# The first norm of a diffusion step: six scale tiles on TensorE ahead of the products, two as row sums on VectorE, the norm's factor applied on GpSimd, loads in another order

## The reference, cut to what matters

```
m = (silu(cond) @ mod_w[i] + mod_b[i]).reshape(.., 9, 1024)        # for c_ctx and for c
x = rms_norm(h, norm_g) * (1 + m[3j+1]) + m[3j]                    # scale, shift
h += 0.5 * m[3j+2] * ((silu(x @ w_gate) * (x @ w_up)) @ w_down)    # hidden width 2816
```

## Time and profile before

| what | us |
|---|---|
| median of 3 runs | 1693.14 (1692.27 to 1697.59) |
| profiled execution | 1691.21 |
| its span | 1689.4 |
| TensorE, matmuls busy | 1616.0 |
| VectorE busy | 1005.7 |
| ScalarE busy | 575.3 |
| GpSimd busy | 84.5 |

### The profile page before, as it was taken

The page is one execution under the profiler, slowest core; times in us unless marked ns, Lnnn a source line. Parts: engine busy times, 40 slices in busy tenths (PEclk is TensorE's granted clock), DMA queues, the critical chain, the costliest instruction groups (busy, mean ns, idle before and its releaser), DMA issues.

```text
span 1689.4 us, 23807 instructions
## 1 busy us (share of the span) xinstructions
PE 1616.0 (96%) x9348; PEld 1559.3 (92%) x9348; DVE 1005.7 (60%) x1338; ACT 575.3 (34%) x738; POOL 84.5 (5%) x48
## 2 busy tenths in 40 slices
PE   5799999989799989999999999998999998999999
PEld 5799999989655889999998999998999998999999
DVE  4667677857645666766875767687755435333323
ACT  3233332252245353323234323213643325232321
POOL 1200000025200010000010000001000000000000
PEclk9599999989779989999998999999999998999999
DMA  9445445625300335454654454466432332333332
GB/s 369 96 175 200 172 174 205 242 80 192 128 0 1 116 121 203 179 194 174 227 196 150 172 201 177 163 233 233 148 142 100 125 125 98 127 124 124 125 124 87
DMA packets 58233, 262.81 MB, mean 156 GB/s; under 512 B 15678, under 2 KB 16574, under 8 KB 36286
## 3 DMA queue, kind: packets, MB, share of 16 engines
q1 hardware_dynamic: 58174, 262.00, 42.9%
HBM read 259.68 MB, written 2.29 MB: 155 GB/s over the span
## 4 chain that ended last, share of the span: by engine, by line
PE 86%; DVE 6%; DMA 3%; issue 2%; ACT 2%; POOL 1%; SPq 0%; POOLq 0%; DVEq 0%; ACTq 0%
PE ps L961 16%; PE ps L962 16%; PE ps L964 16%; PE ps L935 8%; PE ps L936 7%; PE ps L937 7%; DVE mprod L659 3%; DMA raw<-panels 2%; PE ps L974 2%; PE ps L977 2%; PE ps L975 2%; PE ps L1118 2%; PE ps L1023 1%; PE ps L1153 1%; ACT w_hi L459 1%
## 5 line engine op out<-in xcount | busy, mean ns | idle before, releaser
L651 DVE TENSOR_TENSOR w_lo<-raw,w_hi 128x2048 fp32r<-128x2048 f32 x164 | 375.7, 2292 | 294.6 <-ACT w_hi L459 293.8
L961 PE MATMUL ps<-x_hi,w_hi 128*128 128x384 f32 x1536 | 523.9, 341 | 19.5 <-DVE x_lo L729 10.8
L962 PE MATMUL ps<-x_hi,w_lo 128*128 128x384 f32 x1536 | 522.4, 340 | 0.0
L964 PE MATMUL ps<-x_lo,w_hi 128*128 128x384 f32 x1536 | 519.8, 340 | 0.0
L459 ACT ACTIVATE w_hi<-raw 128x2048 fp32r<-128x2048 f32 x169 | 322.9, 1911 | 339.5 <-PE ps L937 191.6
L659 DVE SCALAR_TENSOR_TENSOR mprod<-mraw,cB 128x1024 f32<-128x1024 f32 x256 | 316.9, 1238 | 7.4
L961 PEld LDWEIGHTS ps<-x_hi,w_hi 128*128 128x128 f32 x1536 | 292.4, 190 | 23.4 <-issue 12.1
L962 PEld LDWEIGHTS ps<-x_hi,w_lo 128*128 128x128 f32 x1536 | 292.7, 191 | 0.0
L964 PEld LDWEIGHTS ps<-x_lo,w_hi 128*128 128x128 f32 x1536 | 292.5, 190 | 0.0
L935 PE MATMUL ps<-act_hi,w_hi 128*128 (+1 forms) x832 | 279.8, 336 | 0.3 <-DVE w_lo L651 0.3
L937 PE MATMUL ps<-act_hi,w_lo 128*128 (+1 forms) x832 | 279.7, 336 | 0.0
(11 more groups left out here) (135 smaller groups left out, 1190.0 us busy)
## 6 DMA issues: line engine op xcount, KB each, us to landing
raw<-panels SPq DMA_DIRECT2D x169, 1024.0 KB, 4.8
mraw<-mod_rows SPq DMA_DIRECT2D x128, 512.0 KB, 3.6
mscale<-mod_scale SPq DMA_DIRECT2D x8, 512.0 KB, 15.7
mshift<-mod_rows SPq DMA_DIRECT2D x8, 512.0 KB, 15.9
bias<-toep_scratch SPq DMA_DIRECT2D x32, 64.0 KB, 2.9
h<-x_in_t SPq DMA_DIRECT2D x1, 1536.0 KB, 8.4
out<-h SPq DMA_DIRECT2D x4, 384.0 KB, 2.3
cB<-cond_rows SPq DMA_DIRECT2D x1, 1024.0 KB, 5.4
```

What stands on the lines that cost most here:

```text
L651: nc.vector.tensor_tensor(w_lo[q0 % 2][:, :], raw[q0 % 2][:, :], w_hi[q0 % 2][:, :].bitcast(F32), ALU.subtract).then_inc(lo_done, 1)
L961: mm(out, hi[:, cols], x_hi[:, k, :], start=(k == 0), stop=False)
L962: mm(out, lo[:, cols], x_hi[:, k, :], start=False, stop=False)
L964: last = mm(out, hi[:, cols], x_lo[:, k, :], start=False, stop=(k == KD - 1))
```

## The change

Scale tiles 0 to 5 stay on TensorE and go ahead of all products: tiles 0 and 1 before the sums of squares, tile 2 between them and the spread, tiles 3 to 5 behind it. They lie three to a PSUM bank, and VectorE takes them over in two groups of three (`from_pe`). Scale tiles 6 and 7 become row sums on VectorE (`late`), from rows of `mod_rows`. Shift sums start ahead of the norm (tiles 0 to 2), one stands inside it (tile 3), the others between the splits and the subtractions. [...] Panels 0 and 1 share four tiles of x instead of three. The loads start with scale tile 0 and h, ahead of `cB`; panels 0 and 1 come after k = 3 and k = 5. The row sums write to `mprod0`, which shares its place with the bias, so `load_bias` moves behind pair g0 = 2 and waits for the first sums.

```diff
+PE_TILES = 6
+SUM_TILES = 2 * KD - PE_TILES
@@ SyncE, pair
-                    if f == 0 and g0 == 1:
+                    if f == 0 and g0 == 2:
+                        sp.wait_ge(mchain, 2 * SUM_TILES)
                         load_bias()
@@ SyncE, start
+            def mod_first(k):
+                sp.dma_start(mscale[:, k, :], mod_scale[k] if k < PE_TILES else mod_rows[KD + k]).then_inc(mscale_in[k], 16)
+                sp.dma_start(mshift[:, k, :], mod_rows[k]).then_inc(mshift_in[k], 16)
+
+            sp.dma_start(mscale[:, 0, :], mod_scale[0]).then_inc(mscale_in[0], 16)
+            sp.dma_start(h[:, :, :], x_in_t).then_inc(x_in, 16)
             sp.dma_start(cB[:, :, :], cond_rows.rearrange("(o c) k -> o c k", o=1).to_broadcast([P, 2, D])).then_inc(cb_in, 16)
+            sp.dma_start(mshift[:, 0, :], mod_rows[0]).then_inc(mshift_in[0], 16)
             sp.dma_start(vec[:, :], vecs).then_inc(vec_in, 16)
             sp.dma_start(ident[:, :], consts[0]).then_inc(const_in, 16)
-            sp.dma_start(h[:, :, :], x_in_t).then_inc(x_in, 16)
-            for k in range(KD):
-                sp.dma_start(mscale[:, k, :], mod_scale[k]).then_inc(mscale_in[k], 16)
-                sp.dma_start(mshift[:, k, :], mod_rows[k]).then_inc(mshift_in[k], 16)
-                if k < 2:
-                    panel(k, 0)
+            for k in range(1, KD):
+                mod_first(k)
+                if k in (3, 5):
+                    panel(k // 2 - 1, 0)
@@ GpSimd
             norm(0)
+            pool.wait_ge(r_done, 1)
+            for k in range(KD):
+                if k >= 4:
+                    pool.wait_ge(x_done, k - 3)
+                nc.gpsimd.tensor_tensor(tmp[:, k % 4, :], h[:, k, :], sq[:, 3, :], ALU.mult).then_inc(t_done, 1)
@@ ScalarE
             split(0, 0)
+            act.wait_ge(rb_done, 1)
+            nc.scalar.activation(sq[:, 3, :], ps[:, 5, 0:T], ACT.Copy).then_inc(r_done, 1)
             split(1, 0)
             make_x(0, (0, 0))
@@ VectorE (row_sums waits for a tile's load and calls cond_sums, which now writes to mprod0)
-            rms(0)
+            def first_scale(ks, scale):
+                n = ks.stop - ks.start
+                link(nc.vector.tensor_tensor(aT[:, ks, :], scale, mb1[:, ks, None].to_broadcast([P, n, 2]), ALU.add))
+                nc.vector.tensor_tensor(aT[:, ks, :], aT[:, ks, :], ngT[:, ks, None].to_broadcast([P, n, 2]), ALU.mult) \
+                    .then_inc(mvec, n)
+            def late(k):
+                row_sums(mscale[:, k, :], mscale_in[k], scsum[:, k - PE_TILES, :])
+                shift_sums(k)
+            shift_sums(0)
+            shift_sums(1)
+            shift_sums(2)
+            rms(0, beside=lambda: shift_sums(3))
+            first_shift(slice(0, 4))
+            from_pe(0)
             split(0, 0)
             split(1, 0)
-            make_x(0, first_mod)
+            shift_sums(4)
+            low(0)
+            shift_sums(5)
+            low(1)
+            first_shift(slice(4, 6))
+            from_pe(1)
+            low(2)
+            late(6)
+            late_vectors(6)
+            low(3)
+            low(4)
+            late(7)
+            late_vectors(7)
+            for k in range(5, KD):
+                low(k)
@@ TensorE
-                        project_first(feature_major, q, (0, 2), n,
-                                      (lambda k: mod_scale_tile(k + 1) if 0 < k < KD - 1 else None) if f == 0 else lambda k: None)
+                        project_first(feature_major, q, (0, 2), n, 3 if f else 4)
@@ TensorE, start
+            mod_scale_tile(0)
+            mod_scale_tile(1)
             pe.wait_ge(const_in, 16)
             pe.wait_ge(ones_set, 2)
             norm_sums(0)
+            mod_scale_tile(2)
             norm_spread(0)
-            mod_scale_tile(0)
-            mod_scale_tile(1)
+            for k in range(3, PE_TILES):
+                mod_scale_tile(k)
```

More of the change, by code:

```diff
@@ L82, in build @@
         shsum = sb("shsum", [P, KD, 2])
+        scsum = sb("scsum", [P, KD - PE_TILES, 2])
         cB = sb("cB", [P, 2, D])
@@ L114, in build @@
             svb = sb("svb", [P, KS, T], scope=s)
+        with ExitStack() as s:
+            mprod0 = sb("mprod0", [P, D], scope=s)
         with ExitStack() as s:
@@ L178, in build @@
         rb_done = sem("rb_done")
+        r_done = sem("r_done")
         t_done = sem("t_done")
@@ L298, in mod_block @@
                     if b0 > MOD_FIRST or not isinstance(ii, int):
-                        sp.wait_ge(mchain, 2 * KD + 2 * MT * (b0 - MOD_FIRST - 1) + 2 * a + 2 + 2 * MT * ii)
+                        sp.wait_ge(mchain, 2 * SUM_TILES + 2 * MT * (b0 - MOD_FIRST - 1) + 2 * a + 2 + 2 * MT * ii)
                     sp.dma_start(mraw[a][:, :], mod_rows[bass.ds(MT * (b0 + ii) + a, 1), :, :].rearrange("a p k -> p (a k)")) \
@@ L652, in split, with cond_sums @@
                                         ALU.subtract).then_inc(lo_done, 1)
-            def cond_sums(tile, ii, rows, out):
+            def cond_sums(tile, ii, rows, out, product=mprod):
                 for cond in range(2):
@@ L658, in cond_sums @@
                         dve.wait_ge(mchain, 2 * tile + cond + 2 * MT * ii)
-                    nc.vector.scalar_tensor_tensor(mprod[:, :], rows, 1.0, cB[:, cond, :], ALU.mult, ALU.mult,
+                    nc.vector.scalar_tensor_tensor(product[:, :], rows, 1.0, cB[:, cond, :], ALU.mult, ALU.mult,
                                                    accum_out=out[:, cond:cond + 1]).then_inc(mchain, 1)
@@ L667, in mod_sum @@
                     dve.wait_ge(mraw_in[a], 16 * (n + 1) + 16 * ii)
-                    cond_sums(KD + MT * n + a, ii, mraw[a][:, :], msc[:, a, :])
+                    cond_sums(SUM_TILES + MT * n + a, ii, mraw[a][:, :], msc[:, a, :])
             def mod_out(b0, ii):
-                dve.wait_ge(mchain, 2 * KD + 2 * MT * (b0 - MOD_FIRST + 1) + 2 * MT * ii)
+                dve.wait_ge(mchain, 2 * SUM_TILES + 2 * MT * (b0 - MOD_FIRST + 1) + 2 * MT * ii)
                 nc.vector.tensor_tensor(modT[:, bass.ds(MT * b0 + MT * ii, MT), :], msc[:, :, :],
@@ L693, in gate, with rms @@
                 link(nc.vector.tensor_scalar(gT[:, :, :], modT[:, base:base + KD, :], w, None, ALU.mult))
-            def rms(n, q=None):
+            def rms(n, q=None, beside=lambda: None):
                 def half(a):
@@ L705, in rms @@
                     half(0)
+                beside()
                 dve.wait_ge(rs_done, n + 1)
@@ L711, in rms, with make_x @@
                     half(1).then_inc(lo_done, 1)
-            def make_x(n, beside=lambda k: None):
+            def make_x(n):
                 dve.wait_ge(rb_done, n + 1)
@@ L723, in make_x @@
                 t_of(1)
-                beside(0)
                 for k in range(KD):
-                    if k + 1 < KD:
-                        beside(k + 1)
                     dve.wait_ge(xh_done, KD * n + k + 1)
@@ L774, in _, with row_sums, shift_sums, first_shift @@
             nc.vector.tensor_scalar(mb1[:, :], mbT[:, KD:2 * KD], 1.0, None, ALU.add).then_inc(mod_done, 1)
-            rms(0)
+            dve.wait_ge(cb_done, 1)
+            sums = [0]
+            def row_sums(rows, ready, out):
+                dve.wait_ge(ready, 16)
+                cond_sums(sums[0], 0, rows, out, mprod0)
+                sums[0] += 1
+            def shift_sums(k):
+                row_sums(mshift[:, k, :], mshift_in[k], shsum[:, k, :])
+            def first_shift(ks):
+                dve.wait_ge(mchain, 2 * sums[0])
+                dve.wait_ge(mod_done, 1)
+                nc.vector.tensor_tensor(modT[:, ks, :], shsum[:, ks, :], mbT[:, ks, None].to_broadcast([P, ks.stop - ks.start, 2]),
+                                        ALU.add)
@@ new lines, in first_scale, with from_pe @@
+            def first_scale(ks, scale):
[3 more added lines that the diff above has]
+                    .then_inc(mvec, n)
+            def from_pe(half):
+                ks = slice(PE_TILES // 2 * half, PE_TILES // 2 * half + PE_TILES // 2)
+                dve.wait_ge(mod_pe, PE_TILES // 2 * (half + 1))
+                first_scale(ks, ps[:, 6 + half, 0:PE_TILES].rearrange("p (k c) -> p k c", c=2))
@@ new lines, in low, with late_vectors @@
+            def low(k):
+                dve.wait_ge(xh_done, k + 1)
+                nc.vector.tensor_tensor(x_lo[:, k, :], tmp[:, k % 4, :], x_hi[:, k, :].bitcast(F32), ALU.subtract).then_inc(x_done, 1)
+            def late(k):
+                row_sums(mscale[:, k, :], mscale_in[k], scsum[:, k - PE_TILES, :])
+                shift_sums(k)
+            def late_vectors(k):
+                first_shift(slice(k, k + 1))
+                first_scale(slice(k, k + 1), scsum[:, k - PE_TILES:k - PE_TILES + 1, :])
@@ L946, in mod_scale_tile @@
                 pe.wait_ge(mscale_in[k], 16)
-                if k >= 2:
-                    pe.wait_ge(mvec, k - 1)
+                half, at = divmod(k, PE_TILES // 2)
```

(11 more changed lines are left out.)

## The result

The changed kernel took **1677.1 us** (median of 4 runs, 1675.7 to 1679.6), the kernel before 1694.7 on the same chip (1692.3 to 1697.6): the ratio is 0.990, interval 0.9875 to 0.9919. The profiled executions took 1676.66 and 1691.21, with spans of 1674.9 and 1689.4, so 14.5 us are to be explained; 2.7 were forecast.

A forecast was written before the change was run, and what follows sets the result against it. The prediction took TensorE's matmuls to bound the kernel, busy for 1616.0 of 1689.4 us. Its parts summed as 15.75 - 11.65 - 1.4 = 2.7 us faster, from a median of 1693.1 to 1690.4 us, range 1683 to 1697.

The forecast's parts named there:

- What I cost at nothing: Items given no cost: VectorE's relief from eight products, panel 7, next blocks and later pairs, and the bias's use past 400 us.
- Part 1: At the start, up to ScalarE beginning panel 2's split: the new order brings panel 2's product earlier, gaining 15.75 us.
- the turns: At the start, VectorE and GpSimd operations reading two SBUF operands run one after the other; six GpSimd products cost VectorE 5.9 us.
- the prediction's row: VectorE's work from 35.8 up to the last tile of x: 20.05 us plus 5.9, last scale ready at 61.8.
- p: Moment when panel 0's product ends and ScalarE starts on panel 2: 81.15 before, forecast 66.2.
- The terms of the norm: Listed steps at the start, from the sums of squares through shift tile 3, diagonal and spread, said to end at 30.4.
- Rival B: At the start, GpSimd's products cost VectorE nothing: 5.9 us more gained, 8.6 faster, 1684.5 us; chance 0.18.
- Part 2: Bias loads queued ahead of panel 6, with GpSimd's masks delaying its subtraction: TensorE stalls 11.65 us, ends 7.7 and 13.
- rival A: At panel 6, VectorE's subtraction slips between the two masks: stall 7.7, 6.65 us faster, 1686.5; chance 0.20.
- Rival C: On SyncE behind pair 2, bias issues go slower, 1.13 us each: stall grows 14.9, 12.2 us slower, 1705; chance 0.10.
- Rival D: No stall, panel 6 being in time: 15.75 us faster, 1677; needs the 32 issues under 12.6 us; chance 0.02.
- Part 3: After the stall at panel 6, TensorE runs at half clock for a while: 1.4 us lost, ends 0 and 1.6.

The follow-up runs named there:

- experiment 1: Kernel before with an unused 32- or 64-byte tensor behind `shsum`, and changed kernel with `scsum` allocated last: 1683.2, 1684.6 and 1693.1 us.
- pad32: Kernel before with an unused tensor of 32 bytes per partition behind `shsum`, shifting x and activations but not the weights: 1683.2 us, ratio 0.9918.
- the first set: First of three sets of follow-up runs, each on its own chip with the kernel before in it; that kernel's median there was 1695.5 us.
- experiment 5: Changed kernel with the eight products with the norm's factor put back from GpSimd on VectorE, without ScalarE's copy of the factor: 1676.9 us, ratio 0.9862.
- after_nopad: Changed kernel with its new tensor `scsum` allocated behind all others, so x and weights stand where they stood before: 1693.1 us, ratio 0.9984 to the kernel before.
- w_moved: Kernel before with `msc` and `shsum` allocated ahead of the weights, moving these by 96 bytes and leaving x: 1710.0 us, ratio 1.0056.

## Why the prediction was wrong, point by point

**The step that failed is "What I cost at nothing".** It took "later pairs" as unchanged, with a matmul at before's 0.177 us. The prediction looked at instructions added and moved, and not at the tensor that the diff adds: 16 bytes in the list of allocations. A shift of that kind is worth some 12 us to the kernel before (experiment 1). In the profiled pair of executions it gives 14.5 less the 4 of the start and stall, 10 us; that number belongs to one execution of a kernel that scatters. The number 0.177 was read from the earlier trace rows, one stage; the same view from 620 us on would have shown 0.173, and two paces for one shape under one granted clock would have been a question to ask.

**Part 1 had its order right and its size too small:** 19.3 us against 15.75. `make_x` began at 32.4 (forecast 33.0), the last tile of x came at 59.5 (63.9), the split of panel 2 at 62.9 (66.2). Of those 4.4 us about 2 are the turns: six products were to hold VectorE for 5.9 us; the four sums of 1.9 to 2.0 us from 35 on, one addition of 0.85 at 42.60 and 0.3 in the subtraction at 32.53 show about 4. Another part is that all of the prediction's row came some 1.1 us late into its start: the subtraction of panel 1 began at 32.53, not at 33.6. Some of it was lost again: p came 3.4 us after the last tile of x, where 2.3 were taken (66.2, between the 65.0 and 66.8 that were worked out, without a reason). The terms of the norm that are listed add to 30.2, not 30.4; panel 1's landing at 31.1 hides the difference. And 86.37 is VectorE's product behind pair 0, read as the start of panel 2's product; TensorE's own start of pair 1, 67.19 after the change, lies close to it. Rival B, that the turns cost nothing, was wrong in its premise, and its time of 1684.5 was missed as well.

**Part 2 was right,** issue for issue. 22.4 us for the 32 issues against 21.3, and a stall of about 13 against 11.65, at the upper end given. The masks took 8.95 us together where 8.7 were taken, and the subtraction did not slip between them: rival A did not occur. That the second mask would go ahead of it and hold it to its end, on which 11.65 rests, was the author's estimate from two operations beside the masks (5.43 and 4.33 us); in the run the subtraction was asked for 0.5 us after that mask began, and ended at 114.12, 2.1 after the mask. Rival C needed 0.74 us an issue to turn the sign of the sum; they took 0.70, 22.42 / 32. Rival D named nearly the measured time, 1677, but its mechanism, no stall, did not happen; the time agrees by accident.

**Part 3 was too small:** 2.5 us by the ruler against 1.4. The half clock lasted from 114.2 until after 118, 12 matmuls in 3.8 us, and the stretch behind it was still at 0.85. The term was taken from the nine matmuls at 77.19, and it was more here.

With these sizes the sum of the three parts is 19.3 - 13 - 2.5 = 3.8 faster. That this is near the 2.7 forecast is in part luck: part 1 was 3.6 too small, parts 2 and 3 together 2.5, and the misses offset each other. The ratios don't speak against it: after to before 0.9897, `pad32` to before 0.9918, a difference of 0.2% or 3.6 us, but each with an interval of some 0.2 to 0.3% to either side.

## What to carry to other kernels

Read the list of allocations in a diff as closely as the instructions: a small tensor moves everything behind it, and on a kernel that TensorE bounds, a pace that differs by 2% from stage to stage under the same granted clock (here 176.3 and 173.0 ns at 1.00) says that the layout is worth trying, with an unused tensor of 32 bytes as the first trial (here 1683.2 us against 1695.5). Before a change of some us is judged on such a kernel, look at how far its own executions scatter (before's, 1686.3 to 1706.7 us in the first set). A load that is issued in many pieces belongs where its queue waits anyway (32 bias issues moved there: 10.1 us), and long GpSimd work belongs in pieces behind the VectorE work that TensorE waits for (the subtraction beside the masks: 6.67 us, and 2.29 with pieces of 1.3 us). Work that goes from VectorE to GpSimd can cost VectorE as much as it takes off: here eight products did (experiment 5: 1676.9 us with them on VectorE, 1677.1 on GpSimd).

## What the runs showed of the hardware

- Matmuls of 128x384 follow each other every 173.0 to 173.2, 174.4, 175.3 to 175.7 or 176.3 to 176.5 ns, at a granted clock of 1.00, and moving tensors by some tens of bytes changes which of these occur. Some layouts keep one pace through their trace; others change it from stage to stage, and `after_nopad` changed it at a stall within one loop (191 and 187 matmuls in 32.8 us). No run shows what in the memory is behind it. Seen across layouts, the medians lie 27 us of 1700 apart (`pad32` and `w_moved`, from different sets).
- GpSimd's power for the norm, 1.79 us on a 128x3 tile at 24.37, did not hold VectorE's row sum of 1.23 us at 24.21 and 25.48 in the changed kernel; the prediction had counted 0.8 us for it. GpSimd's products on 128x384 tiles did hold such sums: 2.02 us at 35.03 and 1.92 at 45.10. So the prediction's sentence that such operations run one after the other is shown for products and masks, and not for the power. GpSimd, then VectorE of the changed kernel:

```profile
24.37 1.79 POOL L430 TENSOR_TENSOR rs<-ms,mhalf 128x3 f32<-128x3 f32 x1 [5.38 <-DVE ms L721]
```

```profile
24.21 1.23 DVE L678 SCALAR_TENSOR_TENSOR mprod<-mshift,cB 128x1024 f32<-128x1024 f32 x1
...
25.48 1.23 DVE L678 SCALAR_TENSOR_TENSOR mprod<-mshift,cB 128x1024 f32<-128x1024 f32 x1
```
